# A two-layer attention and mixture-of-experts trunk: the linear attention layer rebuilt, the expert groups interleaved, the last weight part loaded in two halves

## What is computed

```
h = concat(meta, x)                                   # 272 x 1024
h = h + mla_mixer(rms_norm(h))                        # 16-head latent attention, chunk mask
h = h + hier_moe(rms_norm(h))                         # top group of 4, then 2 experts of its 8
h = h + gla_mixer(rms_norm(h))                        # gated linear attention, 4 heads
h = h + hier_moe(rms_norm(h))
return h[16:272]
```

## Time and profile before

| | |
|---|---|
| runs | 798.33, 799.27 and 801.64 us, median 799.27 |
| the profiled execution's own time | 800.42 us |
| its span, first to last instruction | 798.5 us |
| busy share of the span: PE, PE weight loads, DVE, ACT, POOL | 82, 48, 31, 24, 5% |
| chain of waits by engine | PE 66%, DMA 19%, DVE 7%, ACT 3% |
| bytes moved | 233.73 MB, 293 GB/s on average, 420 to 440 GB/s in the stretches where the expert parts stream |
| mean granted TensorE clock | 0.949 |

### The profile page before, as it was taken

The page is one execution under the profiler, slowest core; times in us unless marked ns, Lnnn a source line. Parts: engine busy times, 40 slices in busy tenths (PEclk is TensorE's granted clock), DMA queues, the critical chain, the costliest instruction groups (busy, mean ns, idle before and its releaser), DMA issues.

```text
span 798.5 us, 11424 instructions
## 1 busy us (share of the span) xinstructions
PE 653.3 (82%) x4935; PEld 381.0 (48%) x4935; DVE 243.9 (31%) x511; ACT 194.4 (24%) x355; POOL 39.9 (5%) x45
## 2 busy tenths in 40 slices
PE   5999788958888889887599999769788888577684
PEld 4654565445553455445178444354454544243241
DVE  2137783151332223322414003421333233032031
ACT  2154464442111211121312211242411121021020
POOL 1042000000000000000121002100000000000000
PEclk9999899989999999999799999889979999898897
DMA  9800815555999999999920541509639999999991
GB/s 351 342 1 1 341 82 203 219 210 211 422 439 424 437 426 434 428 434 425 432 124 0 211 157 54 210 1 386 245 123 428 436 425 431 430 428 437 427 423 71
DMA packets 9746, 233.73 MB, mean 293 GB/s; under 512 B 1280, under 2 KB 1600, under 8 KB 2400
## 3 DMA queue, kind: packets, MB, share of 16 engines
q1 hardware_dynamic: 9104, 232.11, 68.7%
q10 hardware_dynamic: 592, 0.87, 0.3%
HBM read 231.92 MB, written 1.05 MB: 292 GB/s over the span
## 4 chain that ended last, share of the span: by engine, by line
PE 66%; DMA 19%; DVE 7%; ACT 3%; issue 3%; POOL 1%; POOLq 0%; DVEq 0%; ACTq 0%
DMA mem<-in_experts 18%; PE ps L794 9%; PE ps L777 8%; PE ps L816 7%; PE ps L576 7%; PE ps L807 6%; PE ps L857 6%; PE ps L848 4%; PE ps L659 4%; PE ps L611 3%; PE ps L601 1%; PE ps L560 1%; DMA mem<-in_early 1%; DVE hT L1453 1%; PE ps L592 1%
## 5 line engine op out<-in xcount | busy, mean ns | idle before, releaser
L794 PE MATMUL ps<-mem,hT 128*32 128x256 f32 x2048 | 114.7, 380 | 5.6 <-DMA mem<-in_experts 5.6
L777 PE MATMUL ps<-mem,xn 128*128 128x128 f32 x640 | 79.8, 287 | 13.8 <-DVE h L1458 12.1
L807 PE MATMUL ps<-mem 128*32 128x512 f32 x512 | 67.5, 675 | 27.5 <-DMA mem<-in_experts 22.9
L777 PEld LDWEIGHTS ps<-mem,xn 128*128 128x128 f32 x640 | 77.3, 202 | 25.8 <-issue 25.8
L794 PEld LDWEIGHTS ps<-mem,hT 128*32 128x32 f32 x2048 | 64.5, 110 | 49.6 <-DMA mem<-in_experts 7.5
L816 PE MATMUL ps<-hT,mem 128*128 128x512 f32 (+1 forms) x160 | 73.3, 600 | 14.5 <-DVE hT L1453 14.5
L1458 DVE TENSOR_TENSOR h<-h,ps 128x512 f32<-128x512 f32 (+1 forms) x80 | 54.7, 684 | 32.4 <-PE ps L816 32.4
L857 PE MATMUL ps<-mem,hT 128*128 128x512 f32 x128 | 56.2, 595 | 0.0
L576 PE MATMUL ps<-mem,hT 128*128 128x512 f32 x128 | 55.7, 593 | 0.0
L816 PEld LDWEIGHTS ps<-hT,mem 128*128 128x128 f32 (+1 forms) x160 | 25.4, 171 | 62.9 <-issue 62.9
L807 PEld LDWEIGHTS ps<-mem 128*32 128x32 f32 x512 | 17.7, 122 | 66.6 <-issue 58.6
(11 more groups left out here) (273 smaller groups left out, 691.9 us busy)
## 6 DMA issues: line engine op xcount, KB each, us to landing
mem<-in_experts SPq DMA_DIRECT2D x48, 4096.0 KB, 27.1
mem<-in_gla_parts SPq DMA_DIRECT2D x4, 4096.0 KB, 31.1
mem<-in_mla_o SPq DMA_DIRECT2D x1, 4096.0 KB, 34.0
mem<-in_mla_w_in SPq DMA_DIRECT2D x2, 1344.0 KB, 10.4
mem<-in_mla_uq SPq DMA_DIRECT2D x1, 2304.0 KB, 20.7
mem<-in_mla_ukv SPq DMA_DIRECT2D x1, 2048.0 KB, 24.8
h<-in_x SPq DMA_DIRECT2D x2, 512.0 KB, 4.5
out<-h SPq DMA_DIRECT2D x2, 512.0 KB, 4.0
```

Of the source, the lines that this page charges most:

```text
L777: mm = pe.matmul(ps[:, k // 4, (k % 4) * P:(k % 4 + 1) * P], xn[:, i, k, :], Sg[:, i, :], start=i == 0, stop=i == nt - 1)
L794: mm = pe.matmul(ps[32 * j:32 * j + 32, 2, m * FE:(m + 1) * FE], xe[:, k, 32 * j:32 * j + 32], w[m][:, j, k * FE:(k + 1) * FE], start=k == ...
L807: mm = pe.matmul(ps[32 * j:32 * j + 32, 5 + b, :], hidT[:, k, 32 * j:32 * j + 32], w[2][:, j, k * D + b * 512:k * D + (b + 1) * 512], star ...
```

## The change

In the expert layers PE's groups are interleaved: while group g's hidden rows are made on ACT and DVE, PE gathers group g+1; the gate part of g+1 is multiplied between the down part and the spreading back of g, and the up part behind it. The gate matrix gets two buffers. The flag is loaded once, ahead of the loop, and the loops over the groups are written out. The last down part of a layer is loaded as two transfers of 2 MB, one for each half of the output columns, and the spreading back of the first half goes ahead of the product of the second. The row norm ahead of linear attention is no longer waited for: PE transposes the raw rows, each row tile as soon as it is added, and the inverse norm is multiplied in when the products are evicted. The inverse root is a power on POOL. The lr job uses four column tiles; a new job s spreads the inverse norms along the rows. The scores of four blocks are made together in four column tiles, with eight buffers instead of three, and two r jobs go behind each half. The attention's end is done for each row tile by itself. The output is stored in four transfers, each behind its own addition. At the start DVE waits for the gains but not for `early`. The diff, cut to its core (bank tables, semaphore names, the slow path's copy of the same steps and the array layouts are left out), first the jobs, the loads and the stores:

```diff
-    JOBS = [("lr", 0, "act", 0)] + [("q", n, "act", 1 + n) for n in range(GH)]
-    JOBS += [("a", n, "dve", (5 + n) % 8) for n in range(GH)] + [("k", n, "act", 1 + n) for n in range(GH)]
-    JOBS += [("v", n, "act", (5 + n) % 8) for n in range(5)] + [("r", n, "act", 4 + n) for n in range(4)]
+    JOBS = [("lr", 0, "dve", 5), ("q", 0, "dve", 7), ("s", 0, "act", 6)] + [("q", n, "dve", n - 1) for n in range(1, GH)]
+    JOBS += [("a", n, "dve", 3 + n) for n in range(GH)] + [("k", n, "dve", (7 + n) % 8) for n in range(GH)]
+    JOBS += [("v", n, "act", (3, 4, 5, 6, 7)[n]) for n in range(5)] + [("r", n, "act", (4, 5, 6, 7)[n]) for n in range(4)]
...
+            if isinstance(g, int) and 3 * g + t == PARTS - 1:
+                sp.dma_start(SLOT[slot][:, 0:HALF], src[:, 0:HALF]).then_inc(half_landed, 16)
+                sp.dma_start(SLOT[slot][:, HALF:], src[:, HALF:]).then_inc(done, 16)
...
+        for b in range(2):
+            for i in range(2):
+                cols = slice(b * 512, (b + 1) * 512)
+                sp.wait_ge(FAST.add, ADD0[1] + 1 + 2 * NT[1] * (GROUPS - 1) + NT[1] * b + i + 1)
+                sp.dma_start(out[0, i * P:(i + 1) * P, cols], h[:, i, cols]).then_inc(stored, 16)
```

POOL, behind `moe_done` and its two memsets:

```diff
-        meta_scaled(2)
-        pool.wait_ge(xn_turned, NB[3])
+        pool.wait_ge(rows_squared, 1)
+        link(pool.tensor_scalar(ssq[:, :], ssq[:, :], EPS, None, ALU.add))
+        link(pool.tensor_tensor(rstd[:, :], ssq[:, :], half_root[:, :], ALU.pow))
+        for j in range(1, 4):
+            ins = pool.tensor_copy(rstd[QUAD * j:QUAD * (j + 1), 2:3], rstd[0:QUAD, 2:3])
...
-            if s >= 3:
-                pool.wait_ge(g_att, s - 2)
-            pool.tensor_tensor(gk[s % 3][:, :, 0:n], gb[:, :, 0:n], ref[:, :, s, :].to_broadcast([P, GH, n]),
+            pool.tensor_tensor(gk[i], gb[:, :, 0:n], ref[:, :, i, :].to_broadcast([P, GH, n]),
                                ALU.subtract).then_inc(gk_dif, 1)
+        for t in range(2):
+            pool.wait_ge(g_osq, t + 1)
+            link(pool.tensor_scalar(gos[:, t], gos[:, t], EPS, None, ALU.add))
+            pool.tensor_tensor(gor[:, t], gos[:, t], half_root[:, 0:1].to_broadcast([P, GH]), ALU.pow).then_inc(g_orstd, 1)
```

PE, the expert groups (`gather` is L777, `gates_turned` L784, `expand` L794, `hidden_turned` L800, `contract` L807 for one half of the columns, `combine` L816 for one half):

```diff
+            gather(FAST, n0)
+            pe.wait_ge(FAST.send, 2 * n0 + 2)
+            gates_turned(FAST)
+            expand(FAST, n0, 0, part(0))
+            expand(FAST, n0, 1, part(1))
+            over_ = overflow(pe, l)
             for g in range(GROUPS):
+                n, last = n0 + g, g == GROUPS - 1
+                pe.wait_ge(FAST.add, ADD0[l] + 1 + 2 * nt * g)
+                if not last:
+                    pe.wait_ge(FAST.send, 2 * n + 3)
+                    gather(FAST, n + 1)
+                hidden_turned(FAST, n)
+                if not last:
+                    pe.wait_ge(FAST.send, 2 * n + 4)
+                    gates_turned(FAST)
+                pe.wait_ge(FAST.hid_c, n + 1)
+                if last:
+                    pe.wait_ge(half_landed, 16 * (l + 1))
+                    contract(FAST, 0, DSLOT[place(l, PARTS - 1)])
+                    combine(FAST, n, 0, PIPED, GT[g % 2])
+                    contract(FAST, 1, part(PARTS - 1))
+                    combine(FAST, n, 1, PIPED, GT[g % 2])
+                else:
+                    w = part(3 * g + 2)
+                    contract(FAST, 0, w)
+                    contract(FAST, 1, w)
+                    expand(FAST, n + 1, 0, part(3 * g + 3))
+                    combine(FAST, n, 0, PIPED, GT[g % 2])
+                    combine(FAST, n, 1, PIPED, GT[g % 2])
+                    expand(FAST, n + 1, 1, part(3 * g + 4))
```

PE, the norm and linear attention:

```diff
-                pe.wait_ge(*(xn_ready(n, i) if n else H_DONE[0][i]))
-                turn(i, xn[:, i] if n else h[:, i, :].rearrange("p (q k) -> p k q", k=KD))
+                pe.wait_ge(*H_DONE[n][i])
+                turn(i, h[:, i, :].rearrange("p (q k) -> p k q", k=KD))
...
+                elif kind == "lr":
+                    for half in range(2):
+                        for m in range(4):
+                            k = HK * half + m
+                            mm = pe.matmul(b[QUAD * m:QUAD * (m + 1), 0:POS], wlr[:, k, :], hT[:, k, :],
+                                           start=half == 0, stop=half == 1)
+                elif kind == "s":
+                    pe.wait_ge(spread_ok, 1)
...
+            def scores(t):
+                pe.wait_ge(gk_ok, 4 * t + 4)
+                for g in range(GH):
+                    for j in range(4):
+                        i = 4 * t + j
+                        n = META + SUB * (i + 1)
+                        mm = pe.matmul(ps[QUAD * j:QUAD * (j + 1), g, 0:n], gqT[:, g, i * SUB:(i + 1) * SUB], gk[i][:, g, :],
+                                       start=True, stop=True)
...
+            scores(0)
+            job(V_END)
+            job(V_END + 1)
+            pe.wait_ge(g_attm, 4)
+            scores(1)
+            job(V_END + 2)
+            job(V_END + 3)
+            pe.wait_ge(g_attm, 8)
...
+            def outputs_turned(t):
+                pe.wait_ge(g_y, t + 1)
...
+            mixer_out(1, wgo, go_done, outputs_turned)
```

`mixer_out` calls `outputs_turned(i)` ahead of row tile i: its eight transposes, and a wait for their evictions. DVE, where `evac` takes the lr, q, a and k jobs (all but a times `spread`):

```diff
+        def norm():
+            for i in range(3):
+                gained(2, i)
+            dve.wait_ge(rows_rstd, 1)
+            for t in range(3):
+                R = WID[t]
+                ins = TS(diag[0:R, COL[t]:COL[t] + R], ident[0:R, 0:R], rstd[0:R, t:t + 1], None, ALU.mult)
+            ins.then_inc(spread_ok, 1)
...
-            dve.wait_ge(in_small, 16 * N_SMALL)
+            dve.wait_ge(in_x0, 48)
             for i in ORDER[0]:
                 gained(0, i)
```

ACT does the eight Exp of `gk` ahead of all evictions of v and r, takes the squares of the output for both row tiles before it evicts a transposed tile, and Ln and Exp are gone:

```diff
-            link(act.activation(flat(gos), flat(gos), ACT.Ln, bias=eps_b))
-            act.activation(flat(gor), flat(gos), ACT.Exp, scale=-0.5).then_inc(g_orstd, 1)
```

More of the change, by code:

```diff
@@ L561, in turn, with mixer_out @@
             mm.then_inc(xn_turned, 1)
-        def mixer_out(l, w, done, ready):
+        def mixer_out(l, w, done, ahead=None):
             n = 2 * l + 1
             for i in range(2):
-                for sem_, v in ready[i]:
-                    pe.wait_ge(sem_, v)
+                if ahead:
+                    ahead(i)
                 for b in range(2):
@@ L822, in moe, with contract, combine @@
-            with pe.If(overflow(pe, l)):
+            def contract(K, b, w):
+                for k in range(2):
+                    for j in range(GE):
+                        mm = pe.matmul(ps[32 * j:32 * j + 32, 5 + b, :], hidT[:, k, 32 * j:32 * j + 32],
+                                       w[:, b, j, k, :], start=k == 0, stop=k == 1)
+                mm.then_inc(K.read, 1)
+            def combine(K, n, b, banks, back):
+                pe.wait_ge(K.turned, n + 1)
+                pe.wait_ge(K.ya if b == 0 else K.yd, n + 1)
+                for i in range(nt):
+                    pe.matmul(ps[0:WID[i], banks[nt * b + i], :], back[:, COL[i]:COL[i] + WID[i]],
+                              ysb[:, b * 512:(b + 1) * 512], start=True, stop=True).then_inc(K.comb, 1)
@@ L823, in moe @@
+            with pe.If(over_):
                 with pe.Fori(0, ROUNDS) as r:
```

498 lines of the change are left out of this document (276 added, 222 removed).

## The result

The changed kernel took 761.51 us, the median of four runs (759.54 to 762.9), against 799.84 us for the kernel before beside it (798.33 to 801.64): **0.951 of its time, 95% interval 0.9478 to 0.9541**. The forecast was 757.3 us, in a range of 750 to 768. So the range held and the sign was right; of 42.0 us forecast, the profiled executions show 39.1 (span 798.5 to 759.4). The agreement of the sums hides that the terms missed both ways. An execution more than 1.5% slower than the fastest of its kernel counts as disturbed and is left out of the ratios; in all that follows this is one execution, of e4.

A forecast was written before the change was run, and what follows sets the result against it. Taken as bound: the expert layers' transfer stream, 190 us from sixth load to last landing, plus PE and short chains between. Seven nonzero terms sum to 42.0 us off 800.42, 758.4 profiled, 757.3 us median; range 750 to 768.

The forecast's parts named there:

- interleaved groups: Expert layers: interleaving removes PE waits of some microseconds a group, but lies under the 10.0 us a part; 0 us.
- start: First projection: DVE evicts tile by tile without waiting for `early`, weights late next by nothing; 2.8 us saved.
- end of layer 0: Behind layer 0's last landing: half products and spreadings bring the last addition to 386.3 us; 4.4 us saved.
- norm ahead of lr: Ahead of linear attention: PE turns raw rows, first product 4.1 us behind the last addition, not 13.3; 9.2 us saved.
- lr and s: Linear attention: lr in column tiles takes 0.9 us, job s adds 0.7 to 1.3; 1.8 us saved.
- scores: Scores with their r jobs: POOL no longer waits for PE, scores take 4.1 us with gaps; 12.6 us saved.
- attention's end: Attention's output: ending by row tile takes 16.9 us, not 24.4, less 2.3 us for tile 1's insert; 5.2 us saved.
- end of layer 1: Behind layer 1's last landing: halves and a last store of a quarter output end the span at 792.5; 6.0 us saved.
- rival of weight loads: Scores and lr: weight loads in column tiles can't be hidden, 8.8 us instead of 4.4, total 762; chance 0.07.
- Late scales: Norm and output: POOL's small steps deliver the scales late, job s holds up PE; 6 us, total 763; chance 0.16.
- Clock: Products behind waits run at the lower clock: down halves, turns, output's first product; 6 us, total 763; chance 0.10.
- A hole in the stream: Expert layers: the down slot is freed late and the load queue runs dry, 5.6 us a group, 835; chance 0.03.

The follow-up runs named there:

- e4: Changed kernel with only the interleaving undone: groups in order again, the last group as in the changed kernel; second run's median 7.9 us above the changed kernel beside it.
- e5: Changed kernel with only the order of the scores' matmuls changed, one column tile at a time; distance between the layers' sixth issues grows by 3.1 us.
- e7: As e1, but PE's turns also wait for the inverse norms, as in the kernel before; 372.9 us between the layers' sixth issues, as in the changed kernel.
- b2: As b1, plus row tile 1's output transposes between the column halves of tile 0's product; 754.91 us, 0.9416 of the kernel before.
- e1: Changed kernel without PE's branch and slow-path copy in layer 0; distance between the layers' sixth issues falls by 3.5 us.
- a_again: The changed kernel, unaltered, measured once more; 765.13 us, 0.9548 of the kernel before.
- b1: Complete changed kernel with PE's branch moved ahead of the last group's gate part, ending in both arms; median 3.6 us above e1's.

## Why the prediction was right, and where its terms were off

The view it rested on held: 190.1 and 190.3 us between sixth issue and last landing, and 189.8 to 190.6 in every experiment and both layers; all gain came from the other stages. Term by term, in us of the profiled executions (the measured column adds up to 39.2, the 39.1 of the spans but for rounding):

```
term                   forecast (bounds)    measured
interleaved groups      0                   0 in the stream, 6 at layer 0's end (in the next rows)
start                   2.8 (0 to 2.8)      1.6
end of layer 0          4.4 (2.5 to 5.2)    1.8
norm ahead of lr        9.2 (7 to 9.8)      4.8
lr and s                1.8 (1 to 2.2)      2.2
scores                 12.6 (9 to 13)      14.2
attention's end         5.2 (3 to 7)        7.3
end of layer 1          6.0 (4.5 to 7)      7.3
```

Three terms came out 8.2 us short and four 5.4 us over. That the sum is so near is luck in part. The end of layer 0, the norm, the scores, the attention's end and the end of layer 1 lie outside their bounds.

*Interleaved groups.* "Worth nothing by itself" is true of the stream and false of its end. The step took the last group's hidden rows for ready at 374.7 us and booked that under the halves; in e4_again, in order and at the lower clock, they are ready only 4.8 us behind the landing. The sum was right since it was in the other term.

*Start.* The weights landed at 11.7 us, not at 10.3. The term took their landing time from the earlier trace rows as fixed; in the thirteen profiles with the change or a variant of it they landed at 11.1 to 11.7 us. Its lower bound covered it.

*End of layer 0.* The down product starts at 374.53 us, but since the stream began 1.6 us earlier, that is 1.4 us later than forecast when both are counted from the sixth issue (187.2 us behind it; 374.7 - 188.9 = 185.8). The up part had landed at 367.6 us, and PE took most of it up only at 368.57, behind the spreading that the interleaving puts ahead of it. Its first half then took 3.55 us and not 1.84, of which the forecast had half. With 0.3 us in the steps behind it this makes the miss of 2.6 us. The 3.55 us are the lower clock (0.53 granted). In e5, whose code is the same up to here, the half took 1.92 us, but it started only 1.3 us ahead of the landing, not 2.9, and the last addition came 10.6 us behind it, as in the profile after (10.7). Only e7 has both the early start and the 1.92 us, and there it is 9.0.

*Norm.* **This is the step that failed**: "PE turns the first tile when its spreading is done". The forecast put the flag's load at nothing and never costed the branch on PE's way from the last spreading to the turns, though the kernel before had it as well: there it lay under the wait for DVE's scaling. lr starts 8.5 us behind the last addition (396.59 - 388.09) where 4.1 were forecast; the term missed by 4.4 us. In b2, without the gap, it is 3.2 us. With the wait for the inverse norms and no branch (e7) it is 9.3. What is late next was asked of POOL, ACT and DVE, and not of PE's own instruction stream.

*Scores.* 0.98 + 1.97 us where 4.1 were taken. The 64 matmuls in four column tiles took 2.95 us, less than 64 times the 0.055 us from the earlier trace rows. The moving sides of the first 32 have 48 to 144 columns and those of the others 176 to 272, where L794's have 256. The rival of weight loads is false: 64 loads of 0.110 us, 7.0 us, lie inside 2.95 us.

```profile
L954 PEld LDWEIGHTS ps<-mem x64: 106/110/110, 459.8 to 476.5; 128*32 128x32 f32 x64
```

So the Trainium skill, "TensorE: Matmul & The Clock Gate", The mechanism, does not describe this case where it lets a weight load overlap running matmuls only if the row group differs: all four column tiles use the same 128 rows, and the order across column tiles halves the time (e5). In the same section the Trainium skill also lets a load for the background weight buffer go ahead; whether that is what happens here no run can tell.

*Attention's end.* 15.0 us where 16.9 were taken. As forecast, ACT's squares of tile 1 stand ahead of its evictions and PE waits for them, 1.92 us. But tile 1's products end 11.9 us behind the scores (502.8 us) where the 13.8 of the earlier trace rows were taken: the granted clock of this stretch is 1.00, and was 0.78 with PE idle in a third of it. The insert of tile 1's transposes costs 1.8 to 2.0 us, of 2.3 forecast. A part of the gain that the forecast did not name is ACT's two table loads, which are no longer there (kernel before):

```profile
531.39 1.28 ACT L1132 ACT_TABLE_LOAD   x1
...
533.00 1.28 ACT L1133 ACT_TABLE_LOAD   x1
```

*End of layer 1.* 8.9 us behind the landing where 10.2 were forecast. The last addition ends 6.4 us behind it (6.2 taken); the rest is the last store, 2.5 us to the end of the span instead of the 4.0 taken.

*The other rivals.* Late scales: false. POOL's steps at the norm took 0.95 and 0.95 (memsets), 0.24, 0.88 and 0.66 us (three copies), and the inverse norms stood at 392.0 us, before the turns were done. In e1 and b2, where the turns come earlier, PE had no wait ahead of job s either:

```profile
390.09 0.24 POOL L555 TENSOR_SCALAR ssq<-ssq 128x3 f32<-128x3 f32 x1
390.42 0.88 POOL L556 TENSOR_TENSOR rstd<-ssq,half_root 128x3 f32<-128x3 f32 x1
391.36 0.66 POOL L558 COPY rstd<-rstd 32x1 f32<-32x1 f32 x3
```

Clock: partly true. The turns took 4.63 us instead of 3.03 and the half product 3.55 instead of 1.92, 3.2 us of the 6; the output's product had the full clock. A hole in the stream: false, the sixth issue to last landing is unchanged.

## What to carry to other kernels

When a wait is taken out, ask also what the engine's own instruction stream does there: a branch round code that is never run cost PE 4 us, unseen as long as a longer wait lay over it, and it cost nothing once it stood ahead of a wait that is there anyway. A part that lies under a transfer stream can still set where the work behind the last landing begins; test "worth 0" at the end of the stream, not in its middle. And where work waits between two stages, keep the clock as a term of its own: 1.6 to 1.8 us for each product that meets the lower level. It came behind idle times of 0.5 to 5.3 us, and behind the same 1.92 us in some profiles and not in others, so one profile can't tell whether a change caused it.

## What was not expected of the hardware

- A taken branch over the slow path, with the DMA share at 1.00: 3.15 to 4.37 us in which PE issues nothing, in all nine profiles that have the branch there. DVE, which loads the flag and branches at the same place, sat idle for 1.03 us there before and did not after.
- A part of the kernel's scatter lies at the start. Between 44 and 60 us the granted clock was 1.00 in some executions and 0.79 to 0.81 in others of the same kernel, with PE busy for all 16.00 us in either. The changed kernel, first its first profile and then a_again:

```profile
44.00:60.00 16.00, 16.00 (x95) 7.16 (x98) 7.30 (x16) 9.67 (x17) 10.71 (x11) 1.00 0.00 1
```

```profile
44.00:60.00 16.00, 16.00 (x77) 7.25 (x72) 5.79 (x14) 8.52 (x17) 8.83 (x9) 0.79 0.00 1
```

  In the chain the same 34 instructions take 14.79 or 17.77 us, and the sixth issue comes 2.9 to 3.7 us later (a_again, e7, b1 and e4_again against the profile after). In a_again the granted clock is 0.50 up to 50.6 us and 1.00 from there. The one profile of the kernel before shows 1.00 there. What decides it was not found: kernels with one and the same start (the changed kernel, e1, e7, b1, e4) fall on either side.
- Interleaved over four column tiles, 32 small matmuls run in half the time that they take tile by tile (1.97 against 4.15 us).
